# Block 2: the last two blocks of down rows taken token tile by token tile, with the next norm's tile-0 transposes inside tile 1's products

## The chip, the cores and the metric

One NeuronCore of one Trainium2 chip runs the whole program. The metric is the device time of one execution in microseconds (us). The engines have their own instruction queues and meet only through semaphores: PE (matmul), ACT (ScalarE), DVE (VectorE), POOL (GpSimd) and SP, which here only issues DMAs.

## The reference

Two transformer-like blocks over 256 tokens of width 1024, all float32. The first (a gated attention and mLSTM mixer, a pooling mixer and two mixtures of experts) isn't touched. The second:

```python
def second_block(x, norms, ...):
    for i in range(2):
        g = norms[i]
        x = x + 0.5 * rms_norm(swiglu(rms_norm(x, g[0]), ffn_wgu[i, 0], ffn_wd[i, 0]), g[1])
        h = rms_norm(x, g[2])
        mix = diff_rwkv_mixer(h, ...) if i % 2 == 0 else retention_mixer(h, ...)
        x = x + rms_norm(mix, g[3])
        x = x + 0.5 * rms_norm(swiglu(rms_norm(x, g[4]), ffn_wgu[i, 1], ffn_wd[i, 1]), g[5])
    return x
# swiglu: gate, up = split(x @ w_gu); (silu(gate) * up) @ w_d, hidden width 2816
```

So there are four FFNs (s = 0 to 3) and two mixers, and between any two layers the same joint: the root mean square of the layer's output y, x += normed y, and the norm of the new x for the next layer.

## The kernel before, in words

**Products.** Float32 operands are split into a high and a low part in the PE's fast float32r form, and each product is three matmuls, high x high, high x low and low x high (`mm3`, whose loop is line 253). Weights are streamed: SP loads a block of 2 MB at most (4096 values a partition) into a ring slot once the slot's earlier block is marked "used" by PE; ACT copies the high part (line 674, two halves) into one of the high buffers, DVE subtracts to get the low part in the slot itself (line 683, two halves). `Parts` plans this: `before` is the block that had the same high buffer, and its "used" mark is what ACT's split waits for; the FFNs have three high buffers, the mixers two. `turn[name]` says which blocks are split in an engine's program at the place of block `name`: up to two ahead. `ready(name)` is DVE's second half. Slots in block 2 are taken in a fixed rotation of four.

**A layer.** FFN s has eleven gate/up blocks ("gu", s, 0..10) and six blocks of down rows ("wd", s, 0), (2), (6), (10), (14), (18), the first of 2 x 128 rows, the others of 4 x 128. Retention has ("ret", 4), ("ret", 0) and on, and its output rows ("out1", 0), (4), (8), (12); the first mixer has ("mix0", 1024), (3072), (2048) and on, and its output ("out0", half). The down products accumulate in PSUM banks 4 to 7, one bank for each token tile t (128 tokens) and half hf of the 1024 columns. Over a block the order is k, t, hf; in the last block it is t, hf, k, so that y(0,0), y(0,1), y(1,0), y(1,1) are finished a quarter of a block apart.

**The seam** (class `Seam`, n = 0 to 6; n = 2 follows the first mixer, n = 6 is the end). For each tile: ACT squares the halves of y out of PSUM (line 486) and takes a root (489, 491), DVE scales y by the norm's row into YG (546) and adds it to X (552, 556), ACT squares X and takes a root, DVE makes a diagonal DG of its reciprocal (561, 563); PE transposes X by eight products with DG (line 616, 16 instructions); ACT makes the high part HH (507) and DVE the low part HL (571). Then PE does the next layer's first block row by row for this tile (`pe_rows`: 625, 626 with HH, 629 with HL, 24 matmuls of 512 columns). The order on PE is transposes 0, rows 0, transposes 1, rows 1, and then the next layer's second block (line 253 with HH, HL).
The order on ACT is sum of y 0, sum of X 0, sum of y 1, high 0, sum of X 1, high 1; at n = 1 the two halves of the split of ("mix0", 1024) stand among these (argument `first`) and high 0 comes before sum of y 1. On DVE it is YG 0, X 0, YG 1, diagonal 0, low 0, X 1, diagonal 1, low 1. `then` is what is split behind all this: ("mix0", 3072) at n = 1 and ("gu", 1, 1) at n = 2. Everywhere else the next layer's first two blocks are split inside the down stage, each when the block two or one before the end is no longer used.

**POOL** computes low parts of the FFN's activations, loads the norm's row for a seam (line 467) and small constants.

Of the kernel before, what the change touches and what calls it, by code (L numbers as in the profile page):

```python
# [13 lines left out]
D = 1024  # L14
# [427 lines left out]
class Seam:  # L442
# [70 lines left out]
    def act(self, a, w, n, half_step, y, at, first=None, then=()):  # L513
# [3 lines left out]
        if first:  # L517
            parts.act(a, w, first, (0,))
        if at is not None:
            self.act_pre(a, w, n, 0, self.x_of(n))  # L520
        if first:
            parts.act(a, w, first, (1,))
            self.act_high(a, w, n, 0, at)
        self.act_post(a, w, n, 1, half_step, y)
        if at is not None:
            if not first:
                self.act_high(a, w, n, 0, at)
            self.act_pre(a, w, n, 1, self.x_of(n))
            self.act_high(a, w, n, 1, at)
# [44 lines left out]
    def dve(self, v, w, n, y, at, first=None, then=()):  # L574
# [3 lines left out]
        if first:  # L578
            parts.dve(v, w, first, (0,))
        else:  # L580
            self.dve_scaled(v, w, n, 1, y)
        if at is None:
            self.dve_x(v, w, n, 1)
            return
        self.dve_diagonal(v, w, n, 0)
        if first:
            parts.dve(v, w, first, (1,))
        self.dve_low(v, w, n, 0, at)
        if first:
            self.dve_scaled(v, w, n, 1, y)  # L590
        self.dve_x(v, w, n, 1)
# [41 lines left out]
class Parts:  # L633
# [29 lines left out]
    def ready(self, name):  # L663
        return self.S.E.at("split_dve", name, 1)
# [1568 lines left out]

def second_loads():
# [9 lines left out]
class Ffn:  # L2244
# [42 lines left out]
    def behind(self, s):  # L2287

        return (("mix0", 1024), ("mix0", 3072)) if s == 0 else ()
# [44 lines left out]
    def pe(self, e, w, s, n):  # L2334
# [4 lines left out]
        for t in range(2):  # L2339
            seam.pe(e, w, n, t)  # L2340
# [26 lines left out]
        for k0, nk in DOWN:  # L2367
            name = ("wd", s, k0)
            wh, wl = S.parts.of(name, nk)
            tail = k0 + nk == 22  # L2370
            order = [(k, t, hf) for t in range(2) for hf in range(2) for k in range(nk)] if tail else [
                (k, t, hf) for k in range(nk) for t in range(2) for hf in range(2)]
            for k, t, hf in order:
                r, c = slice(t * 128, (t + 1) * 128), slice(hf * 512, (hf + 1) * 512)
                w.wait_ge(S.parts.ready(name), self.low(s, k0 + k))
                ins = mm3(e, self.Y[:, 2 * t + hf, :], [(self.AH[:, k0 + k, r], self.AL[:, k0 + k, r], wh[:, k, c], wl[:, k, c])],
                          start=k0 + k == 0, stop=k0 + k == 21)
                if k0 + k == 21:
# [1253 lines left out]
```

## Time and profile before

| | us |
|---|---|
| median of 3 runs | 2582.01 (2579.76 to 2584.98) |
| profiled execution, its span | 2588.0 |
| PE busy | 2124.9 (82%) |
| DVE busy | 915.9 (35%) |
| ACT busy | 742.4 (29%) |

The page gives the time of the profiled execution by its span, from the first to the last instruction. Block 1 takes about the first half and is bound by DMA; block 2 begins about 1320 us after the start. A line of the chain of waits names what was being done or waited for at that time on the way to the last instruction; a line of the timeline gives start, duration, engine and program line, tensor written and tensors read, and in brackets the idle time before it and who ended it.

### The profile page before, as it was taken

The numbers are of one execution on the slowest core, as the hardware profiler recorded it, in microseconds if no ns is written. First come the engines' busy times: TensorE is split into PE (matmuls) and PEld (weight loads), VectorE is DVE, ScalarE is ACT, GpSimd is POOL, SyncE is SP. The second block draws the span as 40 slices with busy tenths as digits, with TensorE's granted clock in tenths as the row PEclk, the third lists the DMA queues.
The fourth block names the chain that finished last, engine by engine and source line by source line (L and its number), as shares of the span: only waits on it lengthen the run. The fifth ranks groups of instructions, "written<-read, shape, count | busy, mean of one in ns | idle before, by whom it ended". The sixth has DMA issues, their size and how long they took to land.

```text
span 2588.0 us, 36096 instructions
## 1 busy us (share of the span) xinstructions
PE 2124.9 (82%) x16306; PEld 1521.9 (59%) x16306; DVE 915.9 (35%) x1325; ACT 742.4 (29%) x1125; POOL 104.3 (4%) x140
## 2 busy tenths in 40 slices
PE   4998876666668766666669998888999999998999
PEld 2764542222224522222249977876998998977997
DVE  4655430000002400000044445546445444445533
ACT  3433310000001200000044444336445444455542
POOL 2100000000000000000001000000100100000010
PEclk8999987788889888888889998989999999999999
DMA  7369789999999499999975543123545645544442
GB/s 276 127 222 387 293 334 425 427 428 427 427 425 383 194 427 428 426 427 428 427 271 179 194 136 112 67 67 114 188 180 171 195 179 187 195 163 138 160 158 107
DMA packets 200025, 679.28 MB, mean 262 GB/s; under 512 B 7952, under 2 KB 101296, under 8 KB 175552
## 3 DMA queue, kind: packets, MB, share of 16 engines
q1 hardware_dynamic: 195328, 664.49, 66.3%
q0 software_dynamic: 2496, 7.24, 0.8%
q10 hardware_dynamic: 2048, 5.24, 0.5%
q8 instruction: 128, 2.10, 0.3%
q14 instruction: 25, 0.20, 0.0%
HBM read 675.90 MB, written 1.05 MB: 262 GB/s over the span
## 4 chain that ended last, share of the span: by engine, by line
PE 54%; DMA 34%; DVE 7%; ACT 4%; issue 1%; SPq 1%; DVEq 0%; ACTq 0%
PE ps L253 42%; DMA ring<-in_w_exp_down 11%; DMA ring<-in_w_exp_gate 11%; DMA ring<-in_w_exp_up 7%; DMA ring<-in_w_mod 4%; PE ps L1862 2%; PE ps L2579 2%; DVE ring_r L683 2%; PE ps L616 1%; PE ps L1877 1%; PE ps L786 1%; PE ps L625 1%; ACT seam_SQ L486 1%; PE ps L626 1%; ACT ring_r L674 1%
## 5 line engine op out<-in xcount | busy, mean ns | idle before, releaser
L253 PE MATMUL ps<-HH,ring_r 128*128 128x256 f32 x2720 | 539.5, 283 | 3.0 <-DVE ring_r L683 3.0
L253 PEld LDWEIGHTS ps<-HH,ring_r 128*128 128x128 f32 x2720 | 438.6, 190 | 6.2 <-DVE ring_r L683 3.6
L1862 PE MATMUL ps<-ring,XS 128*32 128x256 f32 x4096 | 295.6, 440 | 155.2 <-DMA ring<-in_w_exp_gate 108.4
L683 DVE TENSOR_TENSOR ring_r<-ring,ring_r 128x2048 fp32r<-128x2048 f32 (+2 forms) x152 | 326.0, 2186 | 180.4 <-ACT ring_r L674 180.3
L1862 PEld LDWEIGHTS ps<-ring,XS 128*32 128x32 f32 x4096 | 138.6, 123 | 339.0 <-DMA ring<-in_w_exp_gate 162.8
L253 PE MATMUL ps<-HL,ring_r 128*128 128x256 f32 x1136 | 320.9, 282 | 0.0
L674 ACT ACTIVATE ring_r<-ring 128x2048 fp32r<-128x2048 f32 (+2 forms) x152 | 268.7, 1819 | 152.7 <-PE ps L253 94.3
L1877 PE MATMUL ps<-ring,AT 128*32 128x512 f32 x960 | 162.7, 814 | 135.2 <-DMA ring<-in_w_exp_down 132.5
L2086 ACT ACTIVATE SG<-ps 128x256 f32<-128x256 f32 x32 | 12.3, 383 | 819.6 <-PE ps L1862 808.1
L253 PEld LDWEIGHTS ps<-HL,ring_r 128*128 128x128 f32 x1136 | 216.4, 191 | 0.5 <-issue 0.3
L1977 DVE TENSOR_TENSOR AA<-SG,ps 128x256 f32<-128x256 f32 x32 | 13.5, 421 | 518.8 <-PE ps L1862 518.8
L253 PE MATMUL ps<-ring_r,AH 128*128 128x512 f32 x576 | 191.5, 396 | 0.0
L1877 PEld LDWEIGHTS ps<-ring,AT 128*32 128x32 f32 x960 | 31.0, 130 | 242.0 <-DMA ring<-in_w_exp_down 182.6
L683 DVE TENSOR_TENSOR ring_r<-ring,high 128x2048 fp32r<-128x2048 f32 x48 | 107.8, 2288 | 64.3 <-ACT high L674 64.3
L1989 DVE TENSOR_TENSOR OS<-ps,gate 128x512 f32<-128x512 f32 x60 | 38.6, 686 | 258.1 <-PE ps L1877 258.1
L253 PE MATMUL ps<-HH,high 128*128 128x256 f32 x448 | 125.9, 281 | 1.7 <-DVE ring_r L683 1.7
L253 PE MATMUL ps<-HL,high 128*128 128x256 f32 x448 | 126.9, 283 | 0.0
L253 PEld LDWEIGHTS ps<-ring_r,AH 128*128 128x128 f32 x576 | 107.9, 188 | 26.0
L1923 PE MATMUL ps<-OS,GR 128*128 128x512 f32 x240 | 115.9, 627 | 0.4 <-DVE OS L1989 0.4
L674 ACT ACTIVATE high<-ring 128x2048 fp32r<-128x2048 f32 x48 | 89.4, 1913 | 32.6 <-PE ps L253 32.6
L2326 DVE TENSOR_TENSOR ffn_SG<-ffn_SG,ps 128x256 f32<-128x256 f32 x80 | 33.4, 418 | 163.9 <-ACT ffn_SG L2304 163.9
L253 PE MATMUL ps<-ring_r,AL 128*128 128x512 f32 x224 | 88.3, 394 | 0.0
(532 smaller groups left out, 2854.1 us busy)
## 6 DMA issues: line engine op xcount, KB each, us to landing
ring<-in_w_exp_gate SPq DMA_DIRECT2D x64, 2048.0 KB, 35.8
ring<-in_w_exp_up SPq DMA_DIRECT2D x64, 2048.0 KB, 36.1
ring<-in_w_exp_down SPq DMA_DIRECT2D x64, 2048.0 KB, 36.6
ring<-in_ffn_wgu SPq DMA_DIRECT2D x88, 1024.0 KB, 7.7
ring<-in_w_mod SPq DMA_DIRECT2D x24, 2048.0 KB, 13.6
ring<-in_ffn_wd SPq DMA_DIRECT2D x20, 2048.0 KB, 8.0
ring<-in_odd_w_in SPq DMA_DIRECT2D x12, 2048.0 KB, 8.0
ring<-in_even_w_in SPq DMA_DIRECT2D x6, 2048.0 KB, 7.8
```

The lines of the kernel that those rows point to most:

```text
L253: ins = e.matmul(out, l, r, start=start and i == 0, stop=stop and i == n - 1, skip_group_check=True)
L486: a.activation(self.SQ[:, hf, :], src(hf), ACT.Square, accum_out=st[:, hf:hf + 1]).then_inc(*E.up("seam_act", what, n, t, hf))
L616: ins = e.matmul(ps[:, 128 * q:128 * q + 128], S.X[:, t, 128 * k:128 * k + 128], self.DG[:, t, :], start=True, stop=True, skip_group_check ...
L625: e.matmul(out, self.HH[:, k, r], wh[:, k, :], start=k == 0, stop=False, skip_group_check=True)
L674: a.activation(hi[:, c], s[:, c], ACT.Copy).then_inc(*E.up("split_act", name, q))
L683: v.tensor_tensor(lo[:, c], s[:, c], hi[:, c].bitcast(F32), ALU.subtract).then_inc(*E.up("split_dve", name, q))
L1862: ins = e.matmul(self.GU[which][32 * j:32 * j + 32, :], self.XS[:, 4 * hk + k, 32 * n:32 * n + 32], W[:, k, 256 * j:256 * j + 256], start= ...
L1877: ins = e.matmul(self.O[hf][32 * j:32 * j + 32, :], self.AT[:, kk, :], W[:, j, 512 * hf:512 * hf + 512], start=hk == 0, stop=hk == 1, skip ...
L1923: ins = e.matmul(self.Y[:, 2 * t + hf, :], self.GR[:, n, t * 128:(t + 1) * 128], self.OS[:, hf * 512:(hf + 1) * 512], start=n == 0, stop=F ...
L1989: ins = v.tensor_tensor(self.OS[:, sl], self.O[hf], S.gate[:, 1, sl], ALU.mult)
L2326: v.tensor_tensor(sg, sg, ps[:, 256:512], ALU.mult).then_inc(*E.up("ffn_dve", "product", s, f))
L2579: ins = e.matmul(out[h, p, :], l(h, p), q(h, p), start=i == 0, stop=i == len(terms) - 1, skip_group_check=True)
```

## The change

In the four stages that a norm with transposes follows within block 2 and that end in down or output rows (FFN 0, 1, 2 and retention), the last two blocks are taken together: all of tile 0 over both, then all of tile 1. The same order is used in FFN 3. After three of tile 1's four quarters PE does the next seam's transposes of tile 0. ACT and DVE do the whole of tile 0 (high and low parts too) ahead of tile 1's sums, but at n = 2, where only the diagonal of tile 0 moves ahead. The split of the next layer's second block moves behind the seam (`behind`); ("mix0", 1024) is split with the down blocks and loaded into slot 2 instead of 3, and 1536 into slot 3 instead of 2. A down product waits for its half of a block's split only.

```diff
@@ -510,20 +510,18 @@
     def x_of(self, n):
         return lambda t, hf: ("seam_dve", "x", n, t, hf)
 
-    def act(self, a, w, n, half_step, y, at, first=None, then=()):
+    def act(self, a, w, n, half_step, y, at, then=()):
 
         parts = self.S.parts
         self.act_post(a, w, n, 0, half_step, y)
-        if first:
-            parts.act(a, w, first, (0,))
         if at is not None:
             self.act_pre(a, w, n, 0, self.x_of(n))
-        if first:
-            parts.act(a, w, first, (1,))
+        early = at is not None and n != 2
+        if early:
             self.act_high(a, w, n, 0, at)
         self.act_post(a, w, n, 1, half_step, y)
         if at is not None:
-            if not first:
+            if not early:
                 self.act_high(a, w, n, 0, at)
             self.act_pre(a, w, n, 1, self.x_of(n))
             self.act_high(a, w, n, 1, at)
@@ -571,24 +569,21 @@
-    def dve(self, v, w, n, y, at, first=None, then=()):
+    def dve(self, v, w, n, y, at, then=()):
         parts = self.S.parts
         self.dve_scaled(v, w, n, 0, y)
         self.dve_x(v, w, n, 0)
-        if first:
-            parts.dve(v, w, first, (0,))
-        else:
-            self.dve_scaled(v, w, n, 1, y)
+        if at is not None:
+            self.dve_diagonal(v, w, n, 0)
+        early = at is not None and n != 2
+        if early:
+            self.dve_low(v, w, n, 0, at)
+        self.dve_scaled(v, w, n, 1, y)
+        self.dve_x(v, w, n, 1)
         if at is None:
-            self.dve_x(v, w, n, 1)
             return
-        self.dve_diagonal(v, w, n, 0)
-        if first:
-            parts.dve(v, w, first, (1,))
-        self.dve_low(v, w, n, 0, at)
-        if first:
-            self.dve_scaled(v, w, n, 1, y)
-        self.dve_x(v, w, n, 1)
+        if not early:
+            self.dve_low(v, w, n, 0, at)
         self.dve_diagonal(v, w, n, 1)
         self.dve_low(v, w, n, 1, at)
         for name in then:
@@ -660,8 +655,9 @@
-    def ready(self, name):
-        return self.S.E.at("split_dve", name, 1)
+    def ready(self, name, k=None, nk=None):
+        n = self.n[name] // D
+        return self.S.E.at("split_dve", name, 1 if k is None or n < nk else k // 2)
 
+def down_order(blocks):
+
+    for name, first, nk in blocks[:-2]:
+        for k in range(nk):
+            for t in range(2):
+                for hf in range(2):
+                    yield name, first, k, t, hf, (k, t, hf) == (nk - 1, 1, 1)
+    for t in range(2):
+        for name, first, nk in blocks[-2:]:
+            for hf in range(2):
+                for k in range(nk):
+                    yield name, first, k, t, hf, (k, t, hf) == (nk - 1, 1, 1)
+
@@ -2286,7 +2296,7 @@
     def behind(self, s):
 
-        return (("mix0", 1024), ("mix0", 3072)) if s == 0 else ()
+        return ((("mix0", 3072),), (("gu", 2, 1),), (("ret", 0),), ())[s]
@@ -2337,7 +2347,8 @@
         for t in range(2):
-            seam.pe(e, w, n, t)
+            if t or s < 2:
+                seam.pe(e, w, n, t)
...
-        for k0, nk in DOWN:
-            name = ("wd", s, k0)
-            wh, wl = S.parts.of(name, nk)
-            tail = k0 + nk == 22
-            order = [(k, t, hf) for t in range(2) for hf in range(2) for k in range(nk)] if tail else [
-                (k, t, hf) for k in range(nk) for t in range(2) for hf in range(2)]
-            for k, t, hf in order:
-                r, c = slice(t * 128, (t + 1) * 128), slice(hf * 512, (hf + 1) * 512)
-                w.wait_ge(S.parts.ready(name), self.low(s, k0 + k))
-                ins = mm3(e, self.Y[:, 2 * t + hf, :], [(self.AH[:, k0 + k, r], self.AL[:, k0 + k, r], wh[:, k, c], wl[:, k, c])],
-                          start=k0 + k == 0, stop=k0 + k == 21)
-                if k0 + k == 21:
-                    ins.then_inc(*E.up("ffn_pe", "y", s, t, hf))
-                elif (k, t, hf) == order[-1]:
-                    ins.then_inc(*E.up("ffn_pe"))
-            E.alias("ffn_pe", "used", name)
+        for name, first, k, t, hf, leaves in down_order([(("wd", s, k0), k0, nk) for k0, nk in DOWN]):
+            if s < 3 and (first + k, t, hf) == (18, 1, 1):
+                seam.pe(e, w, n + 1, 0)
+            wh, wl = S.parts.of(name, S.parts.n[name] // D)
+            r, c = slice(t * 128, (t + 1) * 128), slice(hf * 512, (hf + 1) * 512)
+            w.wait_ge(S.parts.ready(name, k, 4), self.low(s, first + k))
+            ins = mm3(e, self.Y[:, 2 * t + hf, :], [(self.AH[:, first + k, r], self.AL[:, first + k, r], wh[:, k, c], wl[:, k, c])],
+                      start=first + k == 0, stop=first + k == 21)
+            if first + k == 21:
+                ins.then_inc(*E.up("ffn_pe", "y", s, t, hf))
+            elif leaves:
+                ins.then_inc(*E.up("ffn_pe"))
+            if leaves:
+                E.alias("ffn_pe", "used", name)
         seam.free_banks(n + 1)
@@ -2393,7 +2402,7 @@
-    SLOT_OF = {1024: 3, 3072: 0, 2048: 1, 1536: 2, 2560: 0, 0: 1, 512: 0}
+    SLOT_OF = {1024: 2, 3072: 0, 2048: 1, 1536: 3, 2560: 0, 0: 1, 512: 0}
@@ -2501,7 +2510,8 @@
         for t in range(2):
-            self.seam.pe(e, w, 1, t)
+            if t:
+                self.seam.pe(e, w, 1, t)
@@ -3262,7 +3272,8 @@
         for t in range(2):
-            self.seam.pe(e, w, 4, t)
+            if t:
+                self.seam.pe(e, w, 4, t)
...
-        for k0 in range(0, 16, 4):
-            name = ("out1", k0)
+        for name, first, k, t, hf, leaves in down_order([(("out1", k0), k0, 4) for k0 in range(0, 16, 4)]):
+            if (first + k, t, hf) == (12, 1, 1):
+                self.seam.pe(e, w, 5, 0)
             wh, wl = S.parts.of(name, 4)
-            order = [(k, t, hf) for t in range(2) for hf in range(2) for k in range(4)] if k0 == 12 else [
-                (k, t, hf) for k in range(4) for t in range(2) for hf in range(2)]
...
-            E.alias("ret_pe", "used", name)
+            w.wait_ge(S.parts.ready(name, k, 4), *S.parts_done("ret_dve", ("g",), 16))
+            r, c = slice(t * 128, (t + 1) * 128), slice(hf * 512, (hf + 1) * 512)
+            ins = mm3(e, self.Y[:, 2 * t + hf, :], [(self.QH[:, first + k, r], self.QL[:, first + k, r], wh[:, k, c], wl[:, k, c])],
+                      start=first + k == 0, stop=first + k == 15)
...
@@ -3354,7 +3364,7 @@
         for k0 in range(0, 16, 4):
-            S.parts.dve_next(v, w, ("out1", k0))
+            S.parts.dve_next(v, w, ("out1", k0), ("gu", 3, 1))
...
@@ -3532,15 +3542,15 @@
-        self.seam.act(a, w, 1, True, self.y_of("ffn_pe", 0), 1, *self.ffn.behind(0)[:1], self.ffn.behind(0)[1:])
+        self.seam.act(a, w, 1, True, self.y_of("ffn_pe", 0), 1, self.ffn.behind(0))
         self.rwkv.act(a, w)
         self.seam.act(a, w, 2, False, self.y_of("m0_pe"), 2, then=S.parts.turn["out0", 1])
         self.ffn.act(a, w, 1)
-        self.seam.act(a, w, 3, True, self.y_of("ffn_pe", 1), 3)
+        self.seam.act(a, w, 3, True, self.y_of("ffn_pe", 1), 3, self.ffn.behind(1))
         self.ffn.act(a, w, 2)
-        self.seam.act(a, w, 4, True, self.y_of("ffn_pe", 2), 4)
+        self.seam.act(a, w, 4, True, self.y_of("ffn_pe", 2), 4, self.ffn.behind(2))
         self.ret.act(a, w)
-        self.seam.act(a, w, 5, False, self.y_of("ret_pe"), 5)
+        self.seam.act(a, w, 5, False, self.y_of("ret_pe"), 5, (("gu", 3, 1),))
```
`vector` gets the same arguments as `scalar`, retention's `dve` the same as its `act`.

## Rows read from the trace of the kernel before

**Rows 1.** The page: its first line, and the granted clock in 40 slices.
```profile
span 2588.0 us, 36096 instructions
...
PEclk8999987788889888888889998989999999999999
```
**Rows 2.** Busy time by stretch: stretch, us, each engine's busy us (instructions), clock, DMA share.
```profile
1526.18:1545.63 19.45, 15.28 (x81) 12.62 (x81) 13.62 (x30) 13.29 (x35) 3.68 (x8) 1.00 0.81 281
1775.84:1797.25 21.41, 16.82 (x81) 14.01 (x80) 12.82 (x28) 15.05 (x32) 0.53 (x1) 0.92 0.63 207
1973.35:1992.80 19.45, 16.59 (x82) 14.02 (x81) 10.86 (x27) 12.94 (x31) 0.56 (x1) 0.91 0.41 136
2168.72:2188.18 19.46, 16.62 (x82) 14.24 (x82) 8.86 (x26) 8.55 (x28) 1.08 (x2) 0.91 0.52 189
2384.97:2405.65 20.68, 17.92 (x81) 15.27 (x81) 11.02 (x27) 13.12 (x31) 0.53 (x1) 0.83 0.38 127
...
1797.25:1973.35 176.10, 176.10 (x1228) 163.88 (x1228) 85.69 (x62) 81.33 (x92) 14.77 (x20) 1.00 0.55 185
```
**Rows 3.** PE's waits from 1500 us on: total us, times, longest.
```profile
PE ps L616 <- DVE DG L563: 15.6, 6, 2.9
...
PE ps L253 <- DVE ring_r L683: 3.0, 2, 1.6
```
**Rows 4.** Timeline of PE around seam 3.
```profile
1973.12 0.39 PE L253 MATMUL ps<-ring_r,AL 128*128 128x512 f32 x1
1976.37 2.59 PE L616 MATMUL ps<-DG,X 128*128 128x128 f32 x16 [2.85 <-DVE DG L563]
```
**Rows 5.** Chain of waits in seam 3: start, us, what.
```profile
1985.56 1.78 PE ps L616 x16
...
1991.09 1.87 PE ps L629 x8
```
**Rows 6.** Timeline of all engines, seam 1.
```profile
1520.78 0.60 ACT L486 ACTIVATE seam_SQ<-ps 128x512 f32<-128x512 f32 x1 [1.78 <-PE ps L253]
...
1522.36 1.42 DVE L556 SCALAR_TENSOR_TENSOR X<-YG,seam_st,X 128x512 f32<-128x512 f32 x2
...
1534.59 1.42 DVE L556 SCALAR_TENSOR_TENSOR X<-YG,seam_st,X 128x512 f32<-128x512 f32 x2
...
1537.79 0.30 DVE L563 TENSOR_SCALAR DG<-base,seam_st 128x128 f32<-128x128 f32 x1
```
**Rows 7.** Timeline of all engines, retention's output rows, the last block's split.
```profile
2362.83 3.72 ACT L674 ACTIVATE ring_r<-ring 128x2048 fp32r<-128x2048 f32 x2 [7.48 <-PE ps L253]
2364.78 4.50 DVE L683 TENSOR_TENSOR ring_r<-ring,ring_r 128x2048 fp32r<-128x2048 f32 x2 [6.71 <-ACT ring_r L674]
```
**Rows 8.** Timeline of all engines, seam 2.
```profile
1775.53 0.30 ACT L491 ACTIVATE seam_st<-seam_st 128x1 f32<-128x1 f32 x1
...
1777.74 0.29 ACT L491 ACTIVATE seam_st<-seam_st 128x1 f32<-128x1 f32 x1
...
1788.05 1.95 PE L616 MATMUL ps<-DG,X 128*128 128x128 f32 x16
1788.70 2.17 ACT L507 ACTIVATE HH<-ps,vc 128x128 fp32r<-128x128 f32 x8 [2.19 <-PE ps L616]
1789.35 2.16 DVE L571 SCALAR_TENSOR_TENSOR HL<-ps,vc,HH 128x128 fp32r<-128x128 f32 x8 [2.33 <-ACT HH L507]
1790.71 7.37 ACT L674 ACTIVATE ring_r<-ring 128x2048 fp32r<-128x2048 f32 x4
...
1797.25 0.39 PE L253 MATMUL ps<-HH,ring_r 128*128 128x256 f32 x1 [1.65 <-DVE ring_r L683]
```
**Rows 9.** Chain of waits, the last block of FFN 0.
```profile
1515.17 7.90 DMA ring<-in_even_w_in
```
**Rows 10.** Chain of waits, the end of FFN 3.
```profile
2417.65 164.30 PE ps L253 x1128
```
**Rows 11.** Timeline of PE, seam 5.
```profile
2387.89 3.78 PE L616 MATMUL ps<-DG,X 128*128 128x128 f32 x16 [2.76 <-DVE DG L563]
```

More of the change, by code:

```diff
@@ L3289, in pe @@
             w.wait_ge(*(E.at(*f) for f in B.freed.get(b, ())))
-        for k0 in range(0, 16, 4):
-            name = ("out1", k0)
+        for name, first, k, t, hf, leaves in down_order([(("out1", k0), k0, 4) for k0 in range(0, 16, 4)]):
+            if (first + k, t, hf) == (12, 1, 1):
+                self.seam.pe(e, w, 5, 0)
             wh, wl = S.parts.of(name, 4)
-            order = [(k, t, hf) for t in range(2) for hf in range(2) for k in range(4)] if k0 == 12 else [
-                (k, t, hf) for k in range(4) for t in range(2) for hf in range(2)]
-            for k, t, hf in order:
-                w.wait_ge(S.parts.ready(name), *S.parts_done("ret_dve", ("g",), 16))
-                r, c = slice(t * 128, (t + 1) * 128), slice(hf * 512, (hf + 1) * 512)
-                ins = mm3(e, self.Y[:, 2 * t + hf, :], [(self.QH[:, k0 + k, r], self.QL[:, k0 + k, r], wh[:, k, c], wl[:, k, c])],
-                          start=k0 + k == 0, stop=k0 + k == 15)
-                if k0 + k == 15:
-                    ins.then_inc(*E.up("ret_pe", "y", t, hf))
-                elif (k, t, hf) == order[-1]:
-                    ins.then_inc(*E.up("ret_pe"))
-            E.alias("ret_pe", "used", name)
+            w.wait_ge(S.parts.ready(name, k, 4), *S.parts_done("ret_dve", ("g",), 16))
+            r, c = slice(t * 128, (t + 1) * 128), slice(hf * 512, (hf + 1) * 512)
+            ins = mm3(e, self.Y[:, 2 * t + hf, :], [(self.QH[:, first + k, r], self.QL[:, first + k, r], wh[:, k, c], wl[:, k, c])],
+                      start=first + k == 0, stop=first + k == 15)
+            if first + k == 15:
+                ins.then_inc(*E.up("ret_pe", "y", t, hf))
+            elif leaves:
+                ins.then_inc(*E.up("ret_pe"))
+            if leaves:
+                E.alias("ret_pe", "used", name)
         self.seam.free_banks(5)
@@ L3415, in act @@
         for k0 in range(0, 16, 4):
-            S.parts.act_next(a, w, ("out1", k0))
+            S.parts.act_next(a, w, ("out1", k0), ("gu", 3, 1))
     def act_gates(self, a, w):
@@ L3508, in vector @@
         self.ffn.dve(v, w, 0)
-        self.seam.dve(v, w, 1, self.y_of("ffn_pe", 0), 1, *self.ffn.behind(0)[:1], self.ffn.behind(0)[1:])
+        self.seam.dve(v, w, 1, self.y_of("ffn_pe", 0), 1, self.ffn.behind(0))
         self.rwkv.dve(v, w)
@@ L3512, in vector @@
         self.ffn.dve(v, w, 1)
-        self.seam.dve(v, w, 3, self.y_of("ffn_pe", 1), 3)
+        self.seam.dve(v, w, 3, self.y_of("ffn_pe", 1), 3, self.ffn.behind(1))
         self.ffn.dve(v, w, 2)
-        self.seam.dve(v, w, 4, self.y_of("ffn_pe", 2), 4)
+        self.seam.dve(v, w, 4, self.y_of("ffn_pe", 2), 4, self.ffn.behind(2))
         self.ret.dve(v, w)
-        self.seam.dve(v, w, 5, self.y_of("ret_pe"), 5)
+        self.seam.dve(v, w, 5, self.y_of("ret_pe"), 5, (("gu", 3, 1),))
         self.ffn.dve(v, w, 3)
```

## The prediction

> **What bounds the kernel now.** I read the page first: the span and the slices of granted clock [rows 1]. The program is one chain of layers; the edits lie in block 2, after 1320 us. Next, busy time and clock by stretch [rows 2]. In the FFN stage from 1797.25 to 1973.35 PE is busy for all of its 176.10 us at clock 1.00. The five joints between layers (here called seams, by their norm number n) take 19.45, 21.41, 19.45, 19.46 and 20.68 us from the end of one layer's last product to the first product behind the next layer's first block; four of them run at a mean clock of 0.83 to 0.92. So PE bounds block 2, and only the joints hold time that PE doesn't need. PE's waits [rows 3] name what it idles for there: six waits for the diagonal DG, 15.6 us together, and two for a weight split (DVE, line 683), 3.0 us, both from 1500 us on. PE's own order at seam 3 [rows 4]: the last product starts at 1973.12 (its successor could start 0.23 later, 1973.35), the transposes start at 1976.37, 2.85 us of waiting before them, and take 2.59 us. The chain [rows 5] gives the same pieces at full clock: transposes of a tile 1.78 us, one product of 512 columns 0.2335 us (1.87 for 8), so a tile's 24 row products 5.62 us.
>
> **Units.** One (k, t, hf) of the down products is three matmuls, 0.70 us; a block of four rows is 16 of them, 11.2 us. I put zero, B, at the start of the last two blocks; before, the stage ends at B+22.4, with y(0,0), y(0,1), y(1,0), y(1,1) at 14.0, 16.8, 19.6, 22.4. After the change tile 0's sums are done at 8.4 and 11.2, tile 1's first half at 19.6; there the 1.78 us of transposes stand, and y(1,1) is done at 24.2.
>
> **Part 1: tile 0's transposes inside tile 1's products.** They need DG(0) by B+19.6. Tile 0's norm from y(0,1): at seam 1 ACT starts the square at 1520.78 and DVE the update of X at 1522.36, 1.58 later; tile 1's X at 1534.59 is followed by a DG that ends at 1538.09, 3.50 later [rows 6]. With 0.2 us from product to square that is 5.3 us: DG(0) at B+16.5, 3.1 us early, so PE doesn't wait. ACT must be free by 8.4: the last split ahead of the norm waits for the block two before the end, free at B, and takes 3.7 us on ACT and till 6.5 on DVE (at the last stage of retention two such splits stand there, ACT till 7.4, DVE till 11.1, which delays only the first of two YG; y(0,1) comes at 11.2 anyway). The split that waits for the last block but one (free at 16.8 now) has been put behind the norm in all four stages. Then the next layer's row products of tile 0 (5.62 us) start at B+24.2 with HH and HL ready: high(0) begins 0.7 after the transposes and takes 2.2, HL trails by 0.65, 23.2. Under them runs tile 1's norm, 5.3 us from y(1,1), 0.3 us inside the 5.62. It is the closest margin of the plan; if it is missed, it costs what it is missed by, tenths. So from the old end, T = B+22.4: transposes 1.78, rows 5.62, transposes 1.78, rows 5.62, together 14.80 us, with no idle and hence no fall of the clock.
>
> **Part 2: the last two blocks are used together.** Block 18 (12 in retention) is needed at B+5.6, not 11.2. In the FFNs its high part has a third buffer and its split begins at B-11.2. In retention there are two buffers and it begins at B: ACT at 2362.83, DVE at 2364.78 for two halves in 4.50 [rows 7], with B = 2384.97-22.4 = 2362.57: first half ready at B+4.5, second at B+6.7, by the new wait per half needed at 5.6 and 7.0. No cost; bounds 0 and 1 us.
>
> **Part 3: the deferred split becomes the late one.** At seams 3, 4 and 5 the split of the next layer's second block now stands behind high(1) on ACT. Seam 2 already has this order [rows 8]: transposes of tile 1 start at 1788.05, ACT splits at 1790.71, PE takes the block's first product at 1797.25 after waiting 1.65. (HH at +0.65 for 2.17 us and HL 0.65 behind it, used in part 1, stand there too.) That is 9.20 us from the start of those transposes, where PE alone would need 7.40. So 1.78+5.62+9.20 = 16.60 us from T. Queued behind this split on ACT are the next split, a table load and the SiLU; seam 2 has four splits there in 7.37 us and the stage behind it is the one that is 176.10 of 176.10 busy, so nothing follows.
> Gains: seam 3 19.45-16.60 = 2.85; seam 4 2.86; seam 5 4.08. If the wait disappeared, 1.8 more each; if a second split of 3.7 us were in front, 3.7 less each. I take the middle since a row shows just this queue.
>
> **Part 4: seam 1.** Before, the mixer's first block (mix0 1024) was loaded into the slot that the last block but one leaves: its load lands at 1523.07 after 7.90 us [rows 9], and its two split halves were put between ACT's norm pieces, so PE's rows began late. Now it goes into slot 2, which the block at B-22.4 leaves at B-11.2; it lands about B-3.3, and its split runs at B with the others. The block deferred here is half as wide: of the 9.20 of part 3, 2.66 pass before ACT's split, 1.99 till DVE follows and 4.55 till PE starts; with the latter two halved it is ready 5.9 us after tile 1's transposes start, inside 7.40. So 14.80 us, gain 19.45-14.80 = 4.65. Queue of SP: the next load (2048) waits for the last block and is issued 1.8 us later in the stage while its user comes 4.65 earlier; it lands 8 us after T+1.8, some 5 us ahead. 1536 goes out with it, some 6 us ahead of its split. POOL's constants go out once YG(1,1) is read, as far ahead of their user as before. Cost nothing; bound 2 us.
>
> **Part 5: seam 2** gets only DVE's new order: diagonal(0) no longer stands behind tile 1's scaling. ACT has tile 0's root at 1775.83 [rows 8]; reciprocal and diagonal add 0.5, so transposes start at 1776.4, not 1778.95, after 0.6 us instead of 2.95: the clock stays up. High(0) stands behind tile 1's sum (ACT till 1778.04), first HH at 1778.35, rows 5.62, tile 1's transposes at 1784.0. HL: X(1) now stands before it (till 1779.65), then 2.16 for eight HL [rows 8], 1781.8, needed from 1782.1. 1784.0 against 1788.05 is 4.05 us; all behind it (high(1), split) moves along. Bounds: 2.55 (the wait alone) to 4.3.
>
> **Part 6: the end.** The last FFN has no next norm; y(1,1) comes where it did, and behind it are square, YG, X and the store [rows 10]. Nothing.
>
> **Sum:** 4.65+4.05+2.85+2.86+4.08 = 18.5 us. The profiled execution's time is its span, 2588.0: 2569.5 after. It lies 6.0 above the median of the runs, which I carry over: 2582.0-18.5 = 2563.5.
>
> **A rule on the clock.** At seam 5 PE waits 2.76 us, and then its transposes take 3.78 us, not 1.78 [rows 11]; its window is 2.96 us longer than wait 2.92 + 14.80 explain. That is PE at the lower level, 1.2 GHz, after idling. At seam 3 the second tile's transposes, between products, take 1.78, and PE stays at 2.4. The Trainium skill ("TensorE: Matmul & The Clock Gate", Part 4: PE-mode transpose) says that transposes don't count as activity for this gate. By that rule the 1.78 us inside the products could let the clock fall. The row at seam 3 speaks against it; these transposes are also plain products with a diagonal. It is rival C.
>
> **Rivals.**
> A. Less is saved, 6 to 14 us: DG(1) or HH come late against the 0.3 us margin, or the deferred split costs one more wait per seam, say 3 seams x 1.5 and 1 to 2 at two others. For: margins of tenths. Against: durations here repeat to 0.05 us. Time about 2571.
> B. The late split doesn't come (DMA and DVE free earlier): 3 x 1.8 more, 2558.
> C. The clock falls at the inserted transposes: 3 us at each of four seams, gain 18.5-12 = 6.5, 2575.5.
> D. Slower: tile 0's norm stands behind a split on ACT after all, one that waits for the last block but one. That block is in use until B+16.8; ACT is free at 20.5, DVE's part ends at 23.5, YG x2, X, the second sum and DG follow till 28.4. PE, in order, stands 8.8 us at B+19.6 inside its products, then runs 3 us worse for the low clock; the 1.8 of part 3 is saved: +10 per seam, four seams, 2582.0-18.5+40 = 2603.5. It decides from DG(0) at B+19.6 on, and outweighs the gain when DG(0) is over 7 us late. Against it: the buffers go in turn, so that the first block of the next layer takes that of the block free at B.
> E. No change: the in-order wait eats what the joint saves, DG(0) some 4 us late: 2581.
>
> **Chances.** Forecast 0.76, A 0.08, B 0.03, C 0.03, E 0.04, D 0.06. About 0.2% (5 us) is what a measurement can tell: faster 0.90, same 0.04, slower 0.06. Range: 2556.5 (B, with the spread of the runs shown, 2579.76 to 2584.98) to 2573 (most of A).
>
> **What would show it.** PE without idle from the last down block to the next layer's rows, one group of 16 transposes (line 616) just ahead of the stage's last 12 products; windows of 14.8 (seam 1), 17.4 (seam 2) and 16.6 us (3, 4, 5), clock 1.00 in each; the wait for DG in that stretch down from 15.6 us to about 0.5 (what is left at seam 2), the wait for line 683 up from 3.0 to about 8. A wait for DG inside the down products, or a mean clock under 0.95 in a seam, would prove D, E or C.

## The result, and the profile after

| | before | changed |
|---|---|---|
| median of 4 runs, us | 2582.09 (2579.76 to 2584.98) | 2570.07 (2568.99 to 2571.38) |
| span of the profiled execution | 2588.0 | 2567.2 |

The ratio is 0.995, interval 0.9936 to 0.9964: faster by 12.0 us, inside the range, and 6.6 us above the forecast of 2563.5. The spans of the two traces lie 20.8 us apart, which is nearer to the forecast gain of 18.5 than the medians are. (A run's time is 1.8 us longer than the span of its trace, 2568.99 and 2567.2 here.) That gap is what the experiments had to explain.

The page of the changed kernel, its first line and the granted clock in 40 slices, against [rows 1]:

```profile
span 2567.2 us, 36114 instructions
...
PEclk8999987888789897888879999899999999999999
```
The seams of the changed kernel, in the columns of [rows 2]; a stretch, here called a window, runs from the end of the last product to the first product behind the next layer's row products:

```profile
1525.93:1538.93 13.00, 13.00 (x66) 10.80 (x64) 7.25 (x17) 7.58 (x20) 3.69 (x8) 1.00 0.92 306
1768.06:1784.74 16.68, 15.03 (x81) 12.48 (x80) 12.10 (x26) 13.94 (x30) 0.53 (x1) 1.00 0.80 261
1962.64:1977.44 14.80, 13.15 (x65) 10.61 (x64) 9.34 (x17) 11.59 (x21) 0.56 (x1) 1.00 0.57 186
2155.24:2170.64 15.40, 13.15 (x65) 10.61 (x63) 9.94 (x18) 10.96 (x21) 1.08 (x2) 1.00 0.72 256
2370.01:2384.82 14.81, 13.16 (x65) 10.62 (x63) 9.34 (x17) 11.58 (x21) 0.53 (x1) 1.00 0.56 188
```
The clock is 1.00 in all five, where it was down to 0.83 before, and the four but seam 2 count some 16 PE instructions fewer than before: tile 0's transposes are in the stage ahead. Their 1.78 us belong to the seam in the forecast's way of counting, so the windows to hold against it are 14.78, 16.68, 16.58, 17.18 and 16.59.

What PE waits for from 1480 us on, against [rows 3]. The 15.6 us of waits for DG are gone. The waits for the split (3.0 us, 2 times before) are 6.3 us, 4 times; the two new ones are the late splits of seams 3 and 5. Seam 4's stands in the other group, so that the 8 us of the prediction are 8.5 in the two together:

```profile
PE ps L253 <- DVE ring_r L679: 6.3, 4, 1.7
...
PE ps L253 <- DVE ret_V L3373: 2.2, 1, 2.2
```
Seam 3 of the changed kernel, timeline of all engines (start, duration, engine and line, written, read, idle before), against [rows 4]. Lines 611, 620/621 and 670/679 are the old 616, 625/626 and 674/683.

```profile
1957.81 0.39 PE L253 MATMUL ps<-ring_r,AL 128*128 128x512 f32 x1
1958.03 1.95 PE L611 MATMUL ps<-DG,X 128*128 128x128 f32 x16
1958.68 2.18 ACT L507 ACTIVATE HH<-ps,vc 128x128 fp32r<-128x128 f32 x8 [4.27 <-PE ps L611]
1959.74 0.72 PE L253 MATMUL ps<-ring_r,AH 128*128 128x512 f32 x2
...
1962.64 0.39 PE L620 MATMUL ps<-ring_r,HH 128*128 128x512 f32 x1
...
1962.83 0.60 ACT L486 ACTIVATE seam_SQ<-ps 128x512 f32<-128x512 f32 x1 [0.87 <-PE ps L253]
...
1964.42 1.41 DVE L554 SCALAR_TENSOR_TENSOR X<-YG,seam_st,X 128x512 f32<-128x512 f32 x2
...
1967.63 0.29 DVE L561 TENSOR_SCALAR DG<-base,seam_st 128x128 f32<-128x128 f32 x1
...
1968.23 1.95 PE L611 MATMUL ps<-DG,X 128*128 128x128 f32 x16
...
1970.89 3.77 ACT L670 ACTIVATE high<-ring 128x2048 fp32r<-128x2048 f32 x2
1972.89 4.49 DVE L679 TENSOR_TENSOR ring_r<-ring,high 128x2048 fp32r<-128x2048 f32 x2 [1.19 <-ACT high L670]
...
1977.44 0.39 PE L253 MATMUL ps<-HH,high 128*128 128x256 f32 x1 [1.65 <-DVE ring_r L679]
```
Read PE's lines: the transposes of tile 0 start 0.22 us after the product ahead of them, products go on behind them, rows follow, and no bracket stands on a PE line till the last one. ACT had been idle for 4.27 us before it made the high part, which is how early tile 0's norm was done, and it has HH done at 1960.86. The first idle time of PE is 1.65 us for the deferred split.

### The profile page after: what moved, and what is told of

It is laid out like the page before. It is cut to its first block, busy times and chain, and to the rows that moved or that the text cites. A ratio compares the mean times of both kernels' runs of the same rounds, so it can differ in the third digit from the quotient of the medians.

```text
span 2567.2 us, 36114 instructions
## 1 busy us (share of the span) xinstructions
PE 2108.1 (82%) x16306; PEld 1509.5 (59%) x16306; DVE 915.5 (36%) x1325; ACT 741.7 (29%) x1125; POOL 104.3 (4%) x140
## 4 chain that ended last, share of the span: by engine, by line
PE 55%; DMA 34%; DVE 6%; ACT 3%; SPq 1%; issue 1%; DVEq 0%; ACTq 0%
PE ps L253 44%; DMA ring<-in_w_exp_gate 10%; DMA ring<-in_w_exp_down 10%; DMA ring<-in_w_exp_up 9%; DMA ring<-in_w_mod 4%; PE ps L1858 2%; DVE ring_r L679 2%; PE ps L2589 2%; PE ps L1873 1%; PE ps L782 1%; ACT ring_r L670 1%; PE ps L611 1%; DMA ring<-in_ffn_wgu 1%; SPq L698 1%; PE ps L620 1%
## 6 DMA issues: line engine op xcount, KB each, us to landing
ring<-in_w_mod SPq DMA_DIRECT2D x24, 2048.0 KB, 13.9
```

## Experiments

A ratio is always to the kernel before, timed beside the version in question. There are three groups of versions timed together: e1 to e4 (median of the kernel before 2584.02 us), e5 to e8 (2583.89) and e9 to e12 (2582.57). Times of two versions are compared within a group where that is possible. "Block 2" is the time from seam 0's first transposes to the start of the last update of X in a trace.

**The kernel before once more (e1).** No edit.

> The kernel before once more, unchanged, for its spans and its trace. Block 2 from the first transposes of seam 0 to the last update of X took 1253.5 us in the trace of before (1330.79 to 2584.31) and 1234.1 in that of the change (1329.39 to 2563.46): 19.4 less, though the medians of the runs differ by 12.0 only. Theory A (the profiled execution of before was a long one in block 1): here the span is 2578 to 2583, seam 0 begins at 1321 to 1326, and block 2 again takes 1253.5. Theory B (the edits give 12 in block 2, and the profile exaggerates): block 2 takes about 1246 here and seam 0 begins at 1330.

Measured: 2584.66, ratio 1.0003 (0.9993 to 1.0013). Its trace spans 2582.1, 5.9 less than the one that the prediction used. Theory A had the span right and the place wrong, theory B had the place: block 2's first transposes start at 1330.0 in it and at 1330.8 in the other, and block 2 takes 1248.4 us against 1253.5. The mixer after FFN 0 takes 227.6 against 230.2, and seam 5, timeline of PE, against [rows 11]:

```profile
2384.85 2.05 PE L616 MATMUL ps<-DG,X 128*128 128x128 f32 x16 [2.75 <-DVE DG L563]
```
The same wait (2.75 and 2.76 us), and yet 2.05 us for the transposes where the other execution took 3.78. So the trace that I priced the seams from was, taken together, a long execution in the joints that I priced: its five windows sum to 100.45 us, this one's (20.91, 20.52, 19.47, 19.29, 17.81) to 98.0. Single seams differ both ways. Seam 1 is 1.46 us longer in e1, where tile 1's transposes take 3.52 us instead of 2.05 behind the same wait of 2.65.

**The changed kernel again (e2 and e11).** No edit.

> The changed kernel once more, unchanged, on the same chip. Theory A1 (block 1 varies from run to run only): over the rounds it is 18 to 20 us faster than before, seam 0 begins at the same mean time in both. Theory A2 (block 1 is some 7 us longer in the changed kernel though no line of it was edited): 12 us faster, seam 0 begins about 7 us later than in the kernel before on the same chip. Both: block 2 takes 1234.1.

> The changed kernel a third time, unchanged, beside e9, e10 and e12 on one chip. Theory (give-back by the clock): windows as before to 0.1 us, retention's stage anywhere from 197.5 to 201.5 less the inserted 1.78, ratio to the kernel before 0.995 to 0.996. Rival (the first trace was the typical one): stage 197.6 again and a ratio of 0.993.

Measured: 2570.77, ratio 0.9959 (0.9945 to 0.9974), and 2570.63, ratio 0.9955 (0.9941 to 0.9968). The gain is near A2's 12 us, but not for A2's reason: seam 0 begins at 1328.1 in e2, no later than before, and block 2 takes 1237.1 and 1235.5 us instead of 1234.1. The windows repeat the first trace's to 0.07 us (12.99, 16.72, 14.80, 15.41, 14.80 and 13.00, 16.71, 14.81, 15.41, 14.82). What doesn't repeat is retention. Busy time by stretch, its stage from the first product behind the rows to the last output product; e1's first:

```profile
2185.14:2381.93 196.79, 190.51 (x1001) 157.88 (x999) 94.81 (x84) 98.62 (x119) 0.00 (x0) 1.00 0.46 161
```
the changed kernel in the first trace:

```profile
2170.64:2370.01 199.37, 193.22 (x1017) 161.71 (x1017) 93.82 (x93) 96.06 (x126) 0.00 (x0) 0.99 0.45 157
```
and in e2, with two stretches of it:

```profile
2168.60:2371.83 203.23, 197.23 (x1017) 165.40 (x1017) 93.75 (x93) 96.09 (x126) 0.00 (x0) 0.97 0.44 154
...
2168.60:2188.60 20.00, 20.00 (x154) 20.00 (x155) 9.43 (x5) 7.36 (x9) 0.00 (x0) 0.91 0.54 192
...
2308.60:2328.60 20.00, 14.00 (x57) 10.56 (x56) 14.14 (x27) 11.37 (x27) 0.00 (x0) 0.83 0.18 73
```
Less the inserted 1.78 us the stage takes 197.59, 201.45 and (e11) 199.99 us in the changed kernel, and 196.79 in both traces of before: 0.8, 4.7 and 3.2 us are given back. In e2 the clock is 0.91 in the stage's first 20 us, right behind a wait of 2.24 us, and 0.83 around retention's transposes, where PE waits 2.18 and 2.12. Those transposes show it singly. PE's timeline, the first trace of the changed kernel:

```profile
2315.72 5.38 PE L383 MATMUL ps<-base,ret_G 128*128 128x128 f32 x32 [2.18 <-DVE ret_G L3398]
```
and e1, where the same wait of 2.18 is followed by transposes at full clock:

```profile
2330.10 1.94 PE L383 MATMUL ps<-base,ret_G 128*128 128x128 f32 x16 [2.18 <-DVE ret_G L3388]
2332.34 2.65 PE L383 MATMUL ps<-base,ret_G 128*128 128x128 f32 x16 [0.30 <-DVE ret_QL L434]
```
In e11 the transposes run at full clock too, and yet its stage is 3.2 us longer. There the clock is low at the stage's start, as in e2, and behind the next wait of 2.08 us, at 2322.56, ahead of the output rows. The stretch that holds it:

```profile
2308.98:2328.98 20.00, 13.83 (x59) 9.61 (x60) 13.21 (x26) 10.47 (x24) 0.00 (x0) 0.91 0.13 51
```

**Seam 2 with DVE's old order (e3).**

```diff
         self.dve_x(v, w, n, 0)
-        if at is not None:
+        if n == 2:
+            self.dve_scaled(v, w, n, 1, y)
             self.dve_diagonal(v, w, n, 0)
-        early = at is not None and n != 2
-        if early:
             self.dve_low(v, w, n, 0, at)
-        self.dve_scaled(v, w, n, 1, y)
-        self.dve_x(v, w, n, 1)
+            self.dve_x(v, w, n, 1)
...
```


> The changed kernel with DVE's old order at seam 2 alone (YG 1 ahead of diagonal 0, low 0 ahead of X 1). Prediction's part 5: block 2 4.0 us longer than in the changed kernel, the wait of PE for DG at seam 2 back at 2.95 us and the clock of its window at 0.92. Rival (only the wait counts, the rest is hidden by the late split): 2.5 us longer.

Measured: 2574.25, ratio 0.9965 (0.995 to 0.9979), 3.5 us over e2, with overlapping intervals. Seam 2's window is 21.45 us at clock 0.92, 4.75 more than 16.70; the other four are as in e2. PE's timeline has the pieces, wait and low clock:

```profile
1771.94 3.22 PE L613 MATMUL ps<-DG,X 128*128 128x128 f32 x16 [2.98 <-DVE DG L561]
```
So DVE's order alone (the two instructions of the diagonal ahead of the scaling, low 0 behind X 1) makes seam 2's gain; the rival's 2.5 us is too little. Not all of the 4.75 is its doing. Some 13 to 16 us before seam 2, around the end of a wait of PE of 5.1 us, the granted clock is low for 3.4 us in e3, e6 and the first trace of before, and for 6.8 us in the other eleven traces. In those eleven the last product ends 0.8 us later against ACT's root, and the wait for DG is shorter by as much: 2.14 us in e1, which has DVE's old order too. Its window is 20.52, 3.8 over 16.70. Block 2 is 3.9 us longer than the mean of the three traces of the changed kernel, and the forecast was 4.0.

**Tile 0's transposes behind the last product (e4).**

```diff
-            if s < 3 and (first + k, t, hf) == (18, 1, 1):
-                seam.pe(e, w, n + 1, 0)
...
+        if s < 3:
+            seam.pe(e, w, n + 1, 0)
```
The same in retention.

> The changed kernel with the transposes of tile 0 behind the stage's last product instead of inside tile 1's (four places); token tile order and splits stay. Theory (the place matters through ACT's order: high 0 then stands ahead of tile 1's sums and starts 2.8 us later): high 0 till B+25.3, second square at 26.4, DG of tile 1 at 31.5 against rows that end at 29.8, so 1.7 us of waiting at each of four seams, block 2 6.8 us longer, windows 16.5 at seam 1 and 18.3 at 3, 4 and 5. Rival 1 (PE does the same work in either place, DG of tile 1 comes in time): 0 to 1 us longer. Rival 2 (all of the gain at these seams hangs on the place): 14 us longer.

Measured: 2575.76, ratio 0.997 (0.9958 to 0.9981), 5.0 us over e2. The windows are 16.66, 18.48, 19.08 and 18.48 at seams 1, 3, 4, 5: 1.9 more in each, 7.5 together (forecast 6.8). The wait doesn't vanish with them but goes to tile 1's diagonal. PE, seam 3:

```profile
1978.30 2.05 PE L611 MATMUL ps<-DG,X 128*128 128x128 f32 x16 [1.60 <-DVE DG L561]
```
The theory's reason shows on ACT, same trace and seam:

```profile
1969.78 2.18 ACT L507 ACTIVATE HH<-ps,vc 128x128 fp32r<-128x128 f32 x8 [7.07 <-PE ps L611]
...
1972.05 0.60 ACT L486 ACTIVATE seam_SQ<-ps 128x512 f32<-128x512 f32 x1
```
ACT takes its instructions in order, and high 0 stands ahead of tile 1's sums. It can't start before the transposes, at 1969.14, so ACT squares the second half of tile 1's y at 1973.16 only, 4.0 us after the last product; in the changed kernel (1962.83) it is 0.2 us. The rows and the transposes together would cover tile 1's norm if ACT were free. That place alone makes over half of the 13.9 us that these four windows gained. Block 2 is 6.7 us longer than the mean of the changed kernel (forecast 6.8); the medians, 5.0 apart, have overlapping intervals.

**The deferred split put early (e5 and e12).**

```diff
         if at is not None:
             self.act_pre(a, w, n, 0, self.x_of(n))
         early = at is not None and n != 2
+        if n in (3, 4, 5):
+            for name in then:
+                parts.act(a, w, name)
+            then = ()
```
The same on DVE behind diagonal 0, where low 0 goes behind X 1 at these seams.

> The changed kernel; at seams 3, 4 and 5 the deferred split stands between tile 0's diagonal and its high part instead of behind the whole seam, and DVE takes low 0 behind X 1 there. ACT has nothing from B+16.3 on; the split's buffer is free at B+16.8, so it runs to 20.6 and high 0 starts at 20.6 instead of 20.3; DVE ends it at 23.3. HL of tile 0 is then written from 27.5 on, while the rows need it from 27.9. Theory: the waits of 1.65, 2.25 and 1.65 us for the late split go (and with seam 4's wait the fall of the clock behind it), 0.3 us of waiting for tile 1's diagonal comes in: windows of 13.0 to 13.5 us at seams 3, 4 and 5 against 14.8, 15.4 and 14.8, block 2 about 5 us shorter than in the changed kernel. Rival 1: high 0 or low 0 comes too late and gives the 5 us back, no difference. Rival 2: the split in front of the seam stops ACT as in rival D, slower by 10 or more.

> e5_split_early again, unchanged, beside e11: 5 us under it by the windows (5.4 from the three seams). Rival (e5's ratio of 0.992 was of its chip): the same as e11 within 2 us.

Measured: 2563.54, ratio 0.9923 (0.9909 to 0.9938), and 2563.13, ratio 0.9917 (0.9898 to 0.9937): 7.5 us under e11, which was timed beside it, the fastest version. The windows of seams 3, 4 and 5 are 13.2 in both, 5.4 us less in all. Seam 3 of e5, timeline of all engines:

```profile
1952.14 0.29 DVE L565 TENSOR_SCALAR DG<-base,seam_st 128x128 f32<-128x128 f32 x1
...
1953.00 3.72 ACT L678 ACTIVATE high<-ring 128x2048 fp32r<-128x2048 f32 x2 [1.09 <-PE ps L253]
...
1955.54 1.95 PE L619 MATMUL ps<-DG,X 128*128 128x128 f32 x16
1956.62 2.15 ACT L507 ACTIVATE HH<-ps,vc 128x128 fp32r<-128x128 f32 x8
...
1959.66 0.69 DVE L548 TENSOR_TENSOR YG<-ps,grow 128x512 f32<-128x512 f32 x1 [0.21 <-ACT seam_SQ L486]
...
1960.14 0.39 PE L628 MATMUL ps<-ring_r,HH 128*128 128x512 f32 x1
```
DG is ready 3.1 us before PE wants it. In that gap the block's high buffer comes free, and ACT's split fits between DG and the transposes with HH late by 0.4 us only. Of e12's 7.5 us, 5.4 are windows, the wait for `ret_V` among them, and 1.3 are retention's stage (198.70 against e11's 199.99, each less 1.78); the remaining 0.8 is within the spread of the runs.

**No split behind the norm (e6).**

```diff
-        return ((("mix0", 3072),), (("gu", 2, 1),), (("ret", 0),), ())[s]
+        return ()
```
In retention ("gu", 3, 1) is split with the output rows again.

> The changed kernel without the deferral: in all four stages the split of the next layer's second block stands before the norm, as before the change. Rival D of the prediction made real: ACT waits for the last block but one until B+16.8, is free at 20.5 (18.9 at seam 1, where the block is half as wide), DG of tile 0 comes at 28.4 and PE stands about 8.8 us inside its products, then works at the low clock for a while (3 us), the late split's 1.8 us are saved: windows with the inserted transposes 8 to 10 us longer at each of four seams, block 2 32 to 40 us longer than in the changed kernel, slower than before. Rival (ACT's wait overlaps with PE's products, only the 3.1 us margin is lost): 0 to 8 us longer.

Measured: 2606.66, ratio 1.0086 (1.0063 to 1.0109). PE, seam 3:

```profile
1975.89 3.75 PE L611 MATMUL ps<-DG,X 128*128 128x128 f32 x16 [8.70 <-DVE DG L561]
```
This is rival D: PE stands 8.7 us inside its products (the prediction had 8.8) and the transposes then run at the low clock. At seams 4 and 5 it is 8.7 and 8.6 us, at seam 1 5.7 (the expectation had 8.8 at each of the four), at seam 2 0.4, 32.0 us in all. Block 2 takes 1271.8 us, 36 more than the changed kernel's mean, inside the 32 to 40 expected. The windows at seams 3 to 5 are 13.0, the late split being gone, but the FFN stages in front of them take 186.1 to 189.4 us where the changed kernel's take 177.7 to 178.1, and the retention stage 209.7.

**("mix0", 1024) in its old slot (e7).**

```diff
-    SLOT_OF = {1024: 2, 3072: 0, 2048: 1, 1536: 3, 2560: 0, 0: 1, 512: 0}
+    SLOT_OF = {1024: 3, 3072: 0, 2048: 1, 1536: 2, 2560: 0, 0: 1, 512: 0}
```


> The changed kernel with the old slots of the mixer's blocks (1024 in slot 3, 1536 in slot 2). Theory of part 4: the load of 1024 is then released at B+16.8 and lands at B+24.7, ACT stands at its split ahead of tile 0's norm until 28.4, DVE until 31.2, DG of tile 0 comes at about 36, PE waits some 16 us at B+19.6 and then runs cold: block 2 16 to 20 us longer, all of it at seam 1. Rival (the load lands in time or its split doesn't stop the norm): 0 to 3 us.

Measured: 2588.49, ratio 1.0017 (1.0008 to 1.0027). ACT waits for the load, and PE, in order, for the diagonal behind it; ACT's timeline and PE's in FFN 0:

```profile
1530.78 3.71 ACT L670 ACTIVATE ring_r<-ring 128x2048 fp32r<-128x2048 f32 x2 [32.11 <-DMA ring<-in_even_w_in]
...
1542.16 3.75 PE L611 MATMUL ps<-DG,X 128*128 128x128 f32 x16 [16.52 <-DVE DG L561]
```
That wait alone eats the whole change: block 2 takes 1253.7 us, 18 more than the changed kernel's mean, inside the 16 to 20 expected. The slot is not a detail of part 4 but a condition of it.

**The product order alone (e8).** The kernel before, with `down_order` and the wait per half, nothing else.

> The kernel before with the new order of the last two blocks alone (and the waits per half), nothing inserted, nothing deferred, slots and seams as before. Theory (the order by itself delays the buffer and the slot of the last block but one by 5.6 us, and two splits stand before the norm): the load of 1024 and with it seam 1 5.6 us later; at seams 3, 4 and 5 DG of tile 0 at 28.4 instead of 25.3, 3 us each: block 2 14 to 15 us longer than before. Rival 1 (tile 0's sums come 5.6 us earlier and the norm with them): up to 3 us shorter per seam, 9 in all. Rival 2: no difference.

Measured: 2612.29, ratio 1.0108 (1.0084 to 1.0131). Windows 25.66, 25.79, 25.67 and 25.13 at seams 1, 3, 4, 5. Block 2 takes 1275.2 us, 22 to 27 more than in the two traces of before, where I had expected 14 to 15. I had expected about 3 us each at the last three; against the first trace of before it is 6.3, 6.2 and 4.5. ACT and PE at seam 3:

```profile
1970.30 3.73 ACT L675 ACTIVATE high<-ring 128x2048 fp32r<-128x2048 f32 x2 [13.08 <-PE ps L253]
1973.93 0.57 ACT L486 ACTIVATE seam_SQ<-ps 128x512 f32<-128x512 f32 x1
...
1984.24 3.75 PE L616 MATMUL ps<-DG,X 128*128 128x128 f32 x16 [8.44 <-DVE DG L563]
```
ACT waits for the last block but one, which in this order is used till 5.6 us before the stage's end, splits, and only then squares tile 0's y; the diagonal comes 8.4 us after the last product instead of 2.9. It is e6's mechanism again, and the expectation left out what comes on top: DVE's old order has tile 0's diagonal behind the scaling of tile 1. ACT has tile 0's root at 1981.02, but the diagonal ends at 1984.10, because two scalings of tile 1 stand before it. The order of the products has no worth by itself; it only makes the norm of tile 0 possible earlier, if ACT and DVE are told so.

**PE kept busy in retention (e9 on the changed kernel, e10 on the early split).** Eight products of 512 columns that nothing reads, written to a free bank, stand before retention's transposes and eight before its output rows:

```diff
+        w.wait_ge(*(E.at(*f) for f in B.freed.get(1, ())))
+        self.fill(e, 1)
...
+        self.fill(e, 7)
...
+    def fill(self, e, bank):
+        for _ in range(8):
+            ins = e.matmul(self.S.ps[:, bank, :], self.HH[:, 0, 0:128], self.HH[:, 0:2, :], start=True, stop=True, skip_group_check=True)
+        ins.then_inc(*self.S.E.up("ret_pe"))
```


> The changed kernel with 8 products of 512 columns (1.87 us, results not used) in each of the two waits of PE ahead of and behind retention's transposes (2.2 us and 2.1 to 2.3 us). Retention's stage from the first product behind seam 4 to the last, less the 1.78 us of inserted transposes, took 196.8 in both traces of before and 197.6, 201.4, 198.2 in three of the changed order. Theory (the clock falls in these waits in the changed kernel and gives 1 to 5 us back): with PE kept busy there it takes 196.8 to 197.2 unless the clock falls behind the 2.25 us wait of seam 4, and granted clock is 1.00 in the stage; the median is 1 to 3 us under the changed kernel's. Rival (the stage is longer for another reason, or the added products stand in the way): 198 or more at clock 1.00, or 1 to 4 us longer.

> e5_split_early with the same filling products. No wait over 0.3 us is left between seam 3 and the end but 1.7 us in retention's heads, so theory: retention's stage 196.8 to 197.2 (less 1.78), windows of 13.2 at seams 3 to 5, block 2 from seam 0's first transposes to the last update 1226 to 1228, median 1 to 3 us under e5_split_early. Rival: as for e9.

Measured: e9 2568.65, ratio 0.9937 (0.9917 to 0.9957); e10 2563.64, ratio 0.9916 (0.9895 to 0.9936). The stage and the transposes in e9, busy time by stretch and PE's timeline:

```profile
2170.32:2369.44 199.12, 196.63 (x1033) 163.42 (x1033) 93.46 (x93) 95.98 (x126) 0.00 (x0) 1.00 0.45 157
```
```profile
2315.80 1.97 PE L383 MATMUL ps<-base,ret_G 128*128 128x128 f32 x16 [0.24 <-DVE ret_G L3406]
```
The wait of 2.18 is filled, the clock is 1.00, and the stage less 1.78 takes 197.34 us (e10: 197.25). That is 0.3 to 4.1 us less than in the three traces without the fill. It isn't the 196.8 to 197.2 expected: 0.5 us against before is left at full clock, as in e8, whose stage takes 197.31; what makes it is open. The whole kernel is 2.0 us under e11, with overlapping intervals, and e10 is not under e12 (block 2 takes 1229.3, where 1226 to 1228 was expected). So the two traces point to the clock as the cause of the rest, and no gain of the fill is shown. The wait of 2.24 us at seam 4 stays in e9; that the clock didn't fall behind it there is not the fill's doing.

## Why the prediction came out as it did

The mechanism was right and the size was too large, by 6.5 us of 18.5. Point by point:

- **Part 1, right.** DG(0) costs PE nothing at any seam. DG(1) ends at 1967.92 and PE takes the transposes at 1968.23: inside by 0.3 us, as worked out. Seam 1's 14.78 stands against 14.80. The chain has `L611 x16` at 1958.20 with 1.78 us, so the clock didn't fall at the inserted transposes, there or in any other trace in which PE doesn't wait before them, and rival C is out: the row at seam 3 told more than the rule of the Trainium skill ("TensorE: Matmul & The Clock Gate", Part 4: PE-mode transpose) did here. These are plain float32 products with a diagonal, so the rule itself isn't tested by them.
- **Part 2, right.** No wait stands in the last two blocks; the FFN stages take 176.0 to 176.3 less the inserted 1.78, as before.
- **Part 3, right at seams 3 and 5** (16.58 and 16.59 for 16.60, wait 1.65). **At seam 4 it missed 0.6.** I priced the split by PE's wait alone and left out DVE's queue behind it. The changed kernel, timeline of all engines at seam 4:

```profile
2165.49 4.49 DVE L679 TENSOR_TENSOR ring_r<-ring,ring_r 128x2048 fp32r<-128x2048 f32 x2 [1.20 <-ACT ring_r L670]
...
2169.90 1.28 DVE L3373 COPY ret_V<-ps 128x512 f32<-128x512 f32 x2
2170.64 0.38 PE L253 MATMUL ps<-HH,ring_r 128*128 128x256 f32 x1 [2.25 <-DVE ret_V L3373]
```
  The rows' own evacuation, two copies that free the bank, stands behind the deferred split. The prediction named what is queued behind it on ACT and not what is on DVE.
- **Part 4, right**: the window is 14.78 for 14.80, with e7 showing the price of the other slot. That the gain is 4.67 for 4.65 is in part luck: the window before was 19.45 in that trace and 20.91 in e1.
- **Part 5, right, the gain put 0.7 too small**: the window is 16.68 for 17.4. I had DG 0.6 us after the last product; it is ready at 1767.76, 0.3 before it ends. The root on ACT came 0.8 us earlier against the last product than in [rows 8], and so it does in e1, without the change. It goes with the low clock ahead of this seam, 3.4 us long in the execution of [rows 8] and 6.8 in those of e1 and of the changed kernel (see e3).
- **Part 6, right**: nothing.
- **The sum** of the windows' gains is 18.6 us against the trace that it was made from, where the forecast was 18.5.
- **The step that failed is the one from there to the median.** "It lies 6.0 above the median of the runs, which I carry over" took the surplus of that execution as something that the change leaves alone. (It set a span beside a time; in like terms the surplus is 7.8.) e1 shows that 5.1 of it lay in block 2, 2.5 in the very windows: against e1 they give 98.0 - 81.8 = 16.2 us. The largest piece is seam 5's 2.87 us, with PE at the low clock in one execution and at the full one in the other after the same wait (3.78 or 2.05 us); seam 2 adds 0.89 and seam 1 takes 1.46 back. What a low clock costs in a joint is gained only when it would have been low.
- **And the prediction took what lies outside the seams as unchanged.** The retention stage gives back 0.8 to 4.7 us, 2.9 on the mean of three traces. 16.2 - 2.9 = 13.3, beside 12.0, 13.3 and 11.9 between the medians of the three pairs. The sum leans on e1 as the typical execution, which its time supports (2583.93, with a median of 2584.66); by the mean of both traces of before it would be 17.4 - 2.9 = 14.5. In e2 waits of 2.1 to 2.3 us are followed by a low clock in two places. One of the waits, for `ret_V`, is new with the deferred split; the others stood in the kernel before as well.

What stays open is why the old waits in retention became costly. At the transposes the low clock shows in 6 of the 9 traces of the changed order without a fill. In the other three (e4, e11, e12) it comes behind the next wait, of 2.08 or 2.09 us, so that all 9 have it at one of the two waits at least. None of the 3 traces with the kernel before's seams (before, e1, e8) has it at either, with waits of the same length. Chance alone is a poor explanation of 9 and 0. Neither the inserted transposes nor the deferred split is needed for it: e4 has the transposes outside, and e6 has no deferred split. The product order alone (e8) doesn't bring it. No run tells what does. With both waits filled (e9, e10) the clock stayed high.

Rival A had the time (about 2571) for a partly right reason: "the deferred split costs one more wait" is seam 4's 0.6 and the way into retention. Rivals B, C, D and E didn't come; e6 shows D's mechanism at its predicted size once the deferred split is taken back, and e7 that a split in front of the norm which waits for a load has PE stand 16.5 us.

One part of the change has no run of its own: the new order on ACT and DVE at seams 1, 3, 4 and 5, with high 0 and low 0 ahead of tile 1's sums.

## What to carry to other kernels

Moving work of the next norm into the products pays only if the in-order queues of the other engines are rearranged with it: the product order alone made this kernel 1.1% slower, the change with the old slot 0.2% slower and with a split in front of the norm 0.9% slower, and the whole change 0.5% faster. When a block of ACT or DVE work has to yield, look for the gap where the result is already ready and its user isn't (here 3.1 us between DG and its transposes), rather than the end of the queue: that gave another 7.5 us. And price a joint from more than one execution if PE idles in it: the same wait was followed by transposes of 2.05 or 3.78 us.

## What the runs showed of the hardware

- The same 2.18 us of waiting before retention's 32 transposes was followed by full clock in some executions (1.94 us for the first 16, 2.64 for the others) and by the low one in others (5.4 us for all 32), one kernel showing both (first trace and e11). The granted clock of a stretch is thus no property of the kernel alone where waits of about 2 to 3 us stand in it.
- The seven waits of over 8 us ahead of a seam's transposes in e6, e7 and e8 were all followed by the low level, 3.6 to 3.8 us for 16 of them. The four of 1.60 to 1.63 us in e4 left it high: 2.05 us each.
- Through the 16 inserted transposes of 128 columns, with products right before and behind, the granted clock stayed at 1.00, and they took 1.95 us, in all nine traces that have them so (in e7 at three of the four seams, the fourth having the wait of 16.5 us).
